# Head norms made for a quarter of the columns in four column groups, and attention's matmul visits joined

## The reference

```
q_na = rms_norm(q_na.reshape(B, L, NA_HEADS, NA_HEAD_DIM), lw['q_norm_gain'])
k_na = rms_norm(k_na.reshape(B, L, NA_HEADS, NA_HEAD_DIM), lw['k_norm_gain'])
...
o = rms_norm(o_f + flip(o_b), norm_gain).astype(g.dtype)
def rms_norm(x, gain):
    y = xf * lax.rsqrt(jnp.mean(xf * xf, axis=-1, keepdims=True) + NORM_EPS)
```

## Time and profile before

| | us |
|---|---|
| median of 3 runs | 1637.57 (1637.54 to 1638.14) |
| the profiled execution | 1638.03 |
| its span | 1636.2 |
| PE busy | 1586.0 (97%) |
| DVE busy | 1034.9 (63%) |
| ACT busy | 600.7 (37%) |

### The profile page before, as it was taken

How to read it: one execution, slowest core, us unless ns; L and a number is a source line. 1 busy time by engine, 2 the same in 40 slices (tenths; PEclk the granted TensorE clock), 3 DMA queues, 4 the chain that set the end, 5 groups by cost and what they waited for, 6 DMA issues and landing times.

```text
span 1636.2 us, 29124 instructions
## 1 busy us (share of the span) xinstructions
PE 1586.0 (97%) x12064; PEld 1521.0 (93%) x12064; DVE 1034.9 (63%) x1874; ACT 600.7 (37%) x1101; POOL 428.5 (26%) x177
## 2 busy tenths in 40 slices
PE   4989999999999999999999999999999999999999
PEld 4888888799999999999999888879999999999998
DVE  4574887868885588438788777786777313431432
ACT  4283555444221122212345756554422112221221
POOL 1000000064433344334360000005444333333332
PEclk9899999999999999999999999999999999999999
DMA  9226422124443344234341122312333222222223
GB/s 362 78 95 231 144 85 73 52 64 131 142 151 129 129 150 145 78 109 141 118 128 49 46 88 72 96 41 67 101 116 104 76 77 77 71 71 77 77 64 103
DMA packets 55674, 172.06 MB, mean 105 GB/s; under 512 B 6496, under 2 KB 15520, under 8 KB 55328
## 3 DMA queue, kind: packets, MB, share of 16 engines
q1 hardware_dynamic: 55584, 170.86, 32.6%
HBM read 167.03 MB, written 3.80 MB: 104 GB/s over the span
## 4 chain that ended last, share of the span: by engine, by line
PE 85%; DVE 8%; ACT 3%; issue 1%; DMA 1%; SPq 0%; POOL 0%; DVEq 0%; PEldq 0%; ACTq 0%
PE acc L1427 60%; PE acc L1410 10%; PE acc L1392 6%; PE banks_OX L1638 1%; PE banks_OX L1572 1%; PE bank_S L1540 1%; DMA w_gm<-in_w_ada 1%; PE bank_P L1347 1%; PE bank_P L1557 1%; PE bank_S L1584 1%; PE acc L1557 1%; DVE w_lo L978 1%; PE banks_OX L1478 1%; DVE prob L1247 0%; ACT prob L744 0%
## 5 line engine op out<-in xcount | busy, mean ns | idle before, releaser
L568 POOL TENSOR_TENSOR w_lo<-w_raw,w_hi 128x1024 fp32r<-128x1024 f32 (+1 forms) x152 | 394.1, 2593 | 1191.6 <-ACT w_hi L631 1157.8
L631 ACT ACTIVATE w_hi<-w_raw 128x1024 fp32r<-128x1024 f32 (+2 forms) x194 | 200.2, 1032 | 662.4 <-PE acc L1427 602.6
L1427 PE MATMUL acc<-h_lo,w_hi 128*128 128x320 f32 (+1 forms) x1456 | 336.2, 312 | 0.0
L1427 PE MATMUL acc<-h_hi,w_hi 128*128 128x320 f32 (+1 forms) x1456 | 336.1, 312 | 0.0
L1427 PEld LDWEIGHTS acc<-h_hi,w_hi 128*128 128x128 f32 x1456 | 247.4, 190 | 1.6 <-issue 1.3
L1427 PEld LDWEIGHTS acc<-h_lo,w_hi 128*128 128x128 f32 x1456 | 247.1, 190 | 0.0
L1427 PE MATMUL acc<-h_hi,w_lo 128*128 128x320 f32 (+1 forms) x1456 | 230.3, 310 | 0.0
L1427 PEld LDWEIGHTS acc<-h_hi,w_lo 128*128 128x128 f32 x1456 | 219.7, 189 | 0.0
L1265 DVE SCALAR_TENSOR_TENSOR x<-acc,mods,x 128x320 f32<-128x320 f32 (+2 forms) x192 | 72.6, 434 | 222.4 <-PE acc L1427 200.8
L1427 PE MATMUL acc<-y_lo,w_hi 128*128 128x320 f32 x808 | 184.1, 309 | 0.0
L1427 PE MATMUL acc<-y_hi,w_hi 128*128 128x320 f32 x808 | 184.1, 309 | 0.0
(11 more groups left out here) (256 smaller groups left out, 2222.0 us busy)
## 6 DMA issues: line engine op xcount, KB each, us to landing
w_raw<-in_w SPq DMA_DIRECT2D x176, 512.0 KB, 3.5
mod_w<-in_w_ada SPq DMA_DIRECT2D x56, 512.0 KB, 4.5
w_gm<-in_w_ada SPq DMA_DIRECT2D x24, 512.0 KB, 5.2
bias<-in_bias SPq DMA_DIRECT2D x24, 384.0 KB, 4.1
w_ada<-in_w_ada SPq DMA_DIRECT2D x16, 512.0 KB, 13.7
w_raw<-in_w SPq DMA_DIRECT2D x16, 384.0 KB, 3.1
x<-in_x SPq DMA_DIRECT2D x4, 640.0 KB, 9.4
out_x<-x SPq DMA_DIRECT2D x8, 320.0 KB, 3.9
```

The costliest lines, as they stand in the source:

```text
L568: pool.tensor_tensor(w_lo[p][:, 0:n], raw[p][:, 0:n], w_hi[p][:, 0:n].bitcast(F32), ALU.subtract).then_inc(lo_made[p], 1)
L631: act.activation(w_hi[p][:, 0:n], raw[p][:, 0:n], ACT.Copy).then_inc(hi_made[p], 1)
L1427: mm = pe.matmul(acc[p][:, half, 0:m.shape[-1]], w[:, k * P:(k + 1) * P], m, start=w is w_hi[p] and k == 0 and part is hi, stop=w is w_lo[ ...
```

## The change

- **Sums** (`fill_x`): one fill instead of two. The 640 columns are four quarters of 160, and quarter n is multiplied with 32 columns of `blocks` (16 of each head), into rows 32n to 32n + 31 of bank X, with tile position (0, 32n). So the bank has 160 columns, and the four quarters lie under each other, 16 rows alike for each head.
- **Mean, root, Newton** work on 128x160. They use three pieces of `padded`: `means`, `scratch`, `rs`.
- **Spread** (SP, `spread`): eight transfers for a norm, each one row of `rs` (160 columns) to 64 rows of `means1`, so that it is 128x640 again. DVE waits for `rs_in`, then multiplies as before. Mean, ACT's part and Newton have one DVE or ACT step each; the multiplication is two steps behind Newton, in the same DVE steps as before for queries and keys (10c + 9, 10c + 12).
- **Places in SP's queue**: `spread("q", c)` behind `load(T_PAIR + 3c + 5)`, `spread("k", c)` behind `load(T_PAIR + 3c + 6)`, `spread("g", c)` behind the next; the three biases of a pair are loaded one by one around them.
- **Steps**: the query sum is one PE step earlier, in step 10c + 5, the key sum in 10c + 8, `vtr` in 10c + 11 and 10c + 13.
- **Visits**: `VALUES` is 4, so values fall into the odd steps, and a visit is scores, values, turn, in this order. The loop has one step more (59).

```diff
-TURN, VALUES = 2, 3
+TURN, VALUES = 2, 4
...
-    out += [("vtr", c, i) for c in range(PAIRS) for i in range(2) if step == 10 * c + 11 + i]
-    out += [("gsum", i, h) for i in range(2) for h in range(2) if step == 10 * i + 12 + h]
-    out += [("qsum", c, h) for c in range(PAIRS) for h in range(2) if step == 10 * c + 5 + h]
-    out += [("ksum", c, h) for c in range(PAIRS) for h in range(2) if step == 10 * c + 8 + h]
+    out += [("vtr", c, i) for c in range(PAIRS) for i in range(2) if step == 10 * c + 11 + 2 * i]
+    out += [("gsum", i) for i in range(2) if step == 10 * i + 12]
+    out += [("qsum", c) for c in range(PAIRS) if step == 10 * c + 4]
+    out += [("ksum", c) for c in range(PAIRS) if step == 10 * c + 7]
...
+                def spread(kind, c):
+
+                    sp.wait_ge(rs_made, norms(l, (kind, c)) + 1)
+                    for e in range(2):
+                        for n in range(4):
+                            row = 32 * n + 16 * e
+                            sp.dma_start(means1[64 * e:64 * e + 64, QUARTER * n:QUARTER * (n + 1)],
+                                         rs[row:row + 1, :].unsqueeze(1).broadcast_to([1, 64, QUARTER])).then_inc(rs_in, 16)
...
                     for c in range(PAIRS):
-                        if t == min(T_PAIR + 3 * c + 6, T_OUT - 1):
+                        if t == T_PAIR + 3 * c + 5:
+                            spread("q", c)
+                            if c:
+                                load_bias(c, 0)
+                        if t == T_PAIR + 3 * c + 6:
+                            if c:
+                                load_bias(c, 1)
+                            spread("k", c)
+                            if c:
+                                load_bias(c, 2)
+                        if t == T_PAIR + 3 * c + 7 and c < 2:
+                            spread("g", c)
...
                 def head_newton(name):
 
                     root_of(name)
-                    link(dve.tensor_tensor(means1[:], root[:], root[:], ALU.mult))
-                    link(dve.scalar_tensor_tensor(out=means1[:], in0=means1[:], scalar=-0.5, in1=padded[:, 0:T],
+                    r = root[:, 0:QUARTER]
+                    link(dve.tensor_tensor(scratch, r, r, ALU.mult))
+                    link(dve.scalar_tensor_tensor(out=scratch, in0=scratch, scalar=-0.5, in1=means,
                                                   op0=ALU.mult, op1=ALU.mult))
...
                 def finish_norm(kind, c):
 
-                    link(head_newton((kind, c)))
+                    dve.wait_ge(rs_in, SPREAD * (norms(l, (kind, c)) + 1))
...
-                            pe.matmul(X[:, 0:HALF], blocks, zl[:, int(kind != "qsum"), halves[n]], start=True, stop=True).then_inc(full["X"], 1)
+                            for part in range(4):
+                                rows = slice(32 * part, 32 * part + 32)
+                                mm = pe.matmul(X[rows, 0:QUARTER], blocks[:, 48:80],
+                                               zl[:, int(kind != "qsum"), QUARTER * part:QUARTER * (part + 1)],
+                                               start=True, stop=True, tile_position=(0, 32 * part))
+                            mm.then_inc(full["X"], 1)
...
-                    for c, u in units_at(g, TURN):
-                        turn_probs(c, u)
                     for c, u in units_at(g, 0):
                         scores(c, u)
                     for c, u in units_at(g, VALUES):
                         values(c, u)
+                    for c, u in units_at(g, TURN):
+                        turn_probs(c, u)
```

More of the change, by code:

```diff
@@ L394, in build @@
         squares = padded[:, 0:T]
+        means, scratch, rs = (padded[:, QUARTER * i:QUARTER * (i + 1)] for i in range(3))
         pooled = (root, means1)
@@ L631, in high, with inverse_root @@
                     act.activation(w_hi[p][:, 0:n], raw[p][:, 0:n], ACT.Copy).then_inc(hi_made[p], 1)
-                def inverse_root():
-                    act.activation(root[:], root[:], ACT.Exp, scale=-0.5).then_inc(root_made, 1)
+                def inverse_root(n=T):
+                    act.activation(root[:, 0:n], root[:, 0:n], ACT.Exp, scale=-0.5).then_inc(root_made, 1)
                 def row_roots(name):
@@ L794, in _ @@
                             act.wait_ge(free["X"], 1 + after("X", ("go", NP - 1), l))
+                            act.wait_ge(full["X"], after("X", ("ksum", i), l))
                             act.activation(zl[:, 1, :], gla_o[:, i, :], ACT.Square).then_inc(gla_sq, 1)
```

47 lines of the change are left out of this document (27 added, 20 removed).

## The result

The changed kernel takes **1713.8 us** (median of 4 runs, 1712.0 to 1714.6) against 1637.7 beside it: ratio 1.046, 95% interval 1.0447 to 1.0474. It is 76 us slower. The forecast of 1631 is 83 us off, and the range ended at 1643. Slower had a chance of 0.22; the rival that names the mechanism, B, stood at 1648.

A forecast was written before the change was run, and what follows sets the result against it. PE was taken as the bound, busy 97% of the span and 85% of the last chain. 1638.03 - 20.8 (PE's gains) + 14.0 (layer 0's stall) gave 1631.2, median 0.46 lower, say 1631; range 1623 to 1643.

The forecast's parts named there:

- B: Rival: the spread's round trip is late in every head pair, so scores wait for key norms; 1648, chance 0.20.
- Sums and joined visits: PE's attention part: four-group sums gain 10.8 us, joining scores, values and turn saves 0.2 for each of 40 units, 8.0.
- Rival A: No stall at layer 0's first query norm, so only the gains count: 1617, chance 0.05.
- C: Rival: no change, 1638; shape changes eat the column groups' overlap and joining saves nothing; chance 0.15.
- 8 x 0.48 + 1.6 = 5.4 us: Spread of each norm on SP's queue: eight issues and a landing take 5.4 us.
- the row decides: Spread's landing: the profile row's 1.6 us was taken over the skill page's fixed part of about 2.0 us.
- The steps of a norm are two apart, some 7 us, so most of these fit.: Norm round trips: most fit into the slack of some 7 us; the exception named was layer 0's first query norm.
- The stall of the first query norm: Layer 0: the spread stands behind ctx_k in SP's queue; PE stands 11.3 us at the first 322-column product.
- my 4 to 10: After layer 0's stall, TensorE works 4 to 10 us at half speed.
- the term 14.0: Layer 0's first scores come at 182.6 instead of 168.6: cost 14.0 us, from 11.5 to 17.

The follow-up runs named there:

- no_spread: Changed kernel without the norms' spread transfers and the waits for them, the multiply reading its own rows (normed heads wrong): 1615.2 us.
- sixteen_rows: Changed kernel with the same eight transfers of 64 rows, each reading 16 equal source rows four times instead of one row 64 times: 1673.7 us.
- pool_queue: Changed kernel with all spreads issued by GpSimd instead of SP: 1747.6 us.
- four_dmas: Changed kernel with each spread as four transfers of 128 rows, each reading 32 equal rows four times, instead of eight of 64: 1638.1 us.
- q0_first: Changed kernel with SP's loads of context keys, context values and first biases moved behind layer 0's first query spread: 1704.4 us.
- joined_alone: Kernel before with only the joined visits (scores, values, turn; values one step later), norm and sums as before: 1633.8 us.
- q_not_spread: Changed kernel without the eight query spreads, the query multiply reading its own rows (queries' norm wrong): 1665.8 us.

## Why the prediction was wrong, step by step

- **Sums and joined visits: right.** 0.60 a sum alone against 0.63, 0.24 a unit against 0.20, and 22.5 us in no_spread against 20.8. Rival A's condition, no stall, with every spread hidden, would have been 1617; no_spread runs at 1615. C (groups eaten by changes of shape) falls.
- **"An issue takes 0.43 on SP, a step of 0.48 with the gap, and 64 KB lands 1.6 us later", thus "8 x 0.48 + 1.6 = 5.4 us".** This is the first step that failed. An issue measured 0.60, a step with the gap 0.72, the landing 3.8, and first issue to use 9.1 to 9.2, 3.7 more. Both prices were taken from a transfer of 128 different rows to memory. The pattern here, one row of the chip's own memory read 64 times, has the longer landing, as sixteen_rows shows; with sixteen source rows the landing is 2.2. The page of the Trainium skill (DMA: Bandwidth & Descriptors, Anatomy of one DMA) gives about 2.0 us fixed on GpSimd's path, which would have moved the landing from 1.6 in the right direction, but short of the 3.8 measured from SP and of the 3.7 in pool_queue, on GpSimd's own path. I had written that "the row decides"; it decides only for the pattern that it shows. The sum itself also counts one issue too many, since a landing is timed from the start of its issue: at these prices it is 7 x 0.48 + 1.6 = 5.0.
- **"The steps of a norm are two apart, some 7 us, so most of these fit."** The second that failed. A round trip of 9.1 does not fit into 7, and the sentence treats each by itself. DVE's program puts the query multiply ahead of the keys' Newton steps, so the waits chain: without the queries' spreads PE's key wait falls from 6.36 to 3.15 us in the second pair, and the two kinds are worth 48.0 and 55.1 us. It fails only together with the first step: in four_dmas, where DVE's order is the same and a spread takes 4.9 us, all that is lost against no_spread is 22.9 us.
- **Rival B had the mechanism and not the size.** With the measured e = 9.1 - 5.4 = 3.7 its formula gives 2.5 + 2.8 + 3.7 in layer 1 and 7.4 + 2.8 + 3.7 in layer 0, 22.9, thus 1654. Missing are the queries' share of each pair beyond layer 0's first, and 27.9 us for the clock: B priced a wait as its own length only. I had seen the clock fall after a stall in layer 0 and paid for it once, not behind each of eight key waits. 0.20 was too little for it, and its condition (0.2 us more an issue) was nearer than I held it, with a longest bias issue of 0.99 among the rows.
- **The stall of the first query norm: right in place, mechanism and releaser.** PE stood at the 322-column product for 12.98 us (forecast 11.3), DVE waited 20.45 at that multiply (some 15), SP had the spread behind ctx_k, the biases and a tile, at 165.94:

```profile
161.91 0.33 SPq L512 DMA_DIRECT2D ctx_k<-in_ctx_k  x1
...
165.94 5.71 SPq L487 DMA_DIRECT2D means<-padded  x8
```

```profile
175.01 0.88 DVE L1165 SCALAR_TENSOR_TENSOR qn<-qn,small_all,means 128x640 f32<-128x640 f32 x1 [20.45 <-DMA means<-padded]
```

```profile
176.42 0.64 PE L1440 MATMUL acc<-h_hi,w_hi 128*128 128x322 f32 x1 [12.98 <-DVE shift_cols L997]
```

  PE got there at 163.4, not 160.6: the whole stage began 1.5 us later in this execution, and PE waited 1.9 us more for the row weights, of which I had allowed 0.3. First scores came at 189.3, not 182.6: 4.5 us of that because the stall ended at 176.4 and not at 171.9, and 1.8 as PE's wait for the keys, whose spread took 9.4 us. The clock was low for 7 us of PE's work, inside my 4 to 10. But of the two places from which I had that range only the later shows it: the granted clock is 0.50 from 60 to 73 us, and 1.00 from 31 to 35 us, where I had read half speed from the strides alone. Why products took 0.27 there stays open. The move in q0_first was worth 9.4, the term 14.0.
- **With the spread near the price that I had assumed, the forecast would nearly have held.** In four_dmas a spread takes 4.9 us from first issue to landing (median; 4.1 to 6.9), near my 5.0 to 5.4, and the kernel runs at 1638, 7 above 1631. The seven, and not 83, is about what the rest of the reasoning was off by: against no_spread four_dmas loses 22.9 us where I had 14.0, and its table row shows 11.6 us lost to the clock beyond no_spread's. Part of this agreement is luck, since a better gain (22.5 for 20.8) makes up for some of it.

## What to carry to other kernels

Before moving work from an engine into a round trip by DMA, price the round trip from the same pattern (source rows, number of transfers) and from request to use, and look at what stands behind the waiting instruction in its engine's order: if the next request is made there, the round trips add, and no slack counted for each alone is real. Add for each new wait of TensorE the clock behind it, here about 28 us to 74 of idle time. A few wide transfers from many source rows beat many narrow ones from one row; with the same gains on PE that alone moved this kernel from 4.6% slower to level, and the order of one queue from there to 0.6% faster.

## What the runs showed of the hardware that I had not expected

- A transfer of 40 KB within the chip's own memory that reads one row 64 times lands after 3.8 us; 16 equal rows read four times each, 2.2; 80 KB from 32 rows, 2.9. The issue is about 0.60 us for each of them. Why one source row is slower no run here shows.
- GpSimd's queue issues in 0.53 us, but pauses for 3.8 to 7.9 us after every sixth issue of 64 rows.
- Ten matmuls of no use ahead of each of seven waits made the kernel 8.6 us faster, since the clock gave back more than they overran the waits by (13.1 against 4.1).
- A wait of TensorE of 2.1 us was enough for half clock afterwards in joined_alone at 300 us; the same wait in no_spread's second layer cost nothing, and neither did one of 3.54 us in q_not_spread at 250.6 us, behind which the granted clock stayed at 1.00. The length of a wait alone does not tell what it costs.
